# Second layer's prompt attention: the order of transposes and values on TensorE

## The reference, cut to what matters

```python
def dilated_prompt(q, k, v, slopes):
    outs, lses = [], []
    for gi, (w, r) in enumerate(B_PATTERNS):      # ((128, 1), (512, 4), (2048, 16))
        qs = to_sub(q[:, :, gi], r)[:, :, :, None]
        o, lse = banded_attention(qs, to_sub(k, r), to_sub(v, r), slopes[gi][:, None], r, w // r)
        ...
    return combine_groups(outs, lses)
# banded_attention, in blocks of 128 queries:
#   s = q k^T * HEAD_DIM**-0.5 - slope * distance, masked;  p = exp(s - lse);  o = p v
```

## Time and profile before

| | us |
|---|---|
| median of 3 runs | 2571.18 |
| lowest, highest | 2569.72, 2571.59 |
| the profiled execution | 2568.12 |
| its span | 2566.3 |
| TensorE busy (matmuls) | 2458.2 |
| VectorE busy | 1005.3 |
| ScalarE busy | 657.2 |

### The profile page before, as it was taken

One profiled execution on the slowest core, in us unless ns is written; L12 is line 12 of the kernel. 1 busy time (PEld: TensorE's weight loads), 2 busy tenths in 40 slices (PEclk: granted clock), 3 DMA queues, 4 the chain that ended last, 5 costly groups with the idle time before them and its releaser, 6 DMA issues. The chain is left out here.

```text
span 2566.3 us, 41256 instructions
## 1 busy us (share of the span) xinstructions
PE 2458.2 (96%) x16803; PEld 2369.6 (92%) x16803; DVE 1005.3 (39%) x1911; ACT 657.2 (26%) x1247; POOL 366.7 (14%) x242
## 2 busy tenths in 40 slices
PE   8999899999999999999999997689999999999997
PEld 8887799999999999999999775479999999999997
DVE  6566536322332232236212485436322322323235
ACT  4345324211110111123100493124211111111123
POOL 4333101101100101101111202201101100100100
PEclk9999999999999999999999999899999999999999
DMA  4011214113111313111211233523113111311312
GB/s 173 21 52 36 69 50 141 43 37 120 41 39 56 101 34 121 42 36 49 91 66 35 99 106 102 188 93 115 49 36 107 53 35 47 114 32 54 111 34 85
DMA packets 64943, 186.72 MB, mean 73 GB/s; under 512 B 11288, under 2 KB 17816, under 8 KB 64056
## 3 DMA queue, kind: packets, MB, share of 16 engines
q1 hardware_dynamic: 63928, 180.46, 21.7%
q0 software_dynamic: 912, 4.85, 0.5%
HBM read 175.85 MB, written 44.70 MB: 86 GB/s over the span
## 5 line engine op out<-in xcount | busy, mean ns | idle before, releaser
L969 DVE TENSOR_TENSOR WL<-RAW,WH 128x1024 fp32r<-128x1024 f32 (+3 forms) x196 | 216.4, 1105 | 1147.7 <-ACT WH L632 1147.1
L1508 PE MATMUL PS<-XH,WH 128*128 128x384 f32 x2832 | 621.0, 329 | 5.5 <-DVE XL L996 3.2
L1508 PE MATMUL PS<-XH,WL 128*128 128x384 f32 (+1 forms) x2736 | 603.5, 328 | 0.0
L1508 PE MATMUL PS<-XL,WH 128*128 128x384 f32 x2640 | 581.7, 328 | 0.0
L1508 PEld LDWEIGHTS PS<-XH,WH 128*128 128x128 f32 x2832 | 484.0, 188 | 7.3 <-issue 4.3
L632 ACT CAST WH<-RAW 128x1024 fp32r<-128x1024 f32 (+3 forms) x196 | 184.8, 944 | 1164.0 <-PE PS L1508 1149.1
L1508 PEld LDWEIGHTS PS<-XH,WL 128*128 128x128 f32 x2736 | 467.6, 188 | 0.0
L496 POOL TENSOR_TENSOR RAW<-RAW,GAIN 128x1024 f32<-128x1024 f32 x112 | 225.9, 2019 | 1663.7 <-DMA RAW<-in_w_gu 1418.7
L1508 PEld LDWEIGHTS PS<-XL,WH 128*128 128x128 f32 x2640 | 450.7, 188 | 0.0
L1508 PE MATMUL PS<-HL,WH 128*128 128x384 f32 (+1 forms) x1041 | 228.6, 327 | 0.0
L1508 PE MATMUL PS<-HH,WL 128*128 128x384 f32 (+1 forms) x1041 | 228.5, 327 | 0.0
(11 more groups left out here) (222 smaller groups left out, 2355.5 us busy)
## 6 DMA issues: line engine op xcount, KB each, us to landing
RAW<-in_w_gu SPq DMA_DIRECT2D x88, 512.0 KB, 3.5
out_bkS<-in_bk_in SPq DMA_DIRECT2D x8, 2032.0 KB
out_bvS<-in_bv_in SPq DMA_DIRECT2D x8, 2032.0 KB
RAW<-in_w_dn SPq DMA_DIRECT2D x32, 384.0 KB, 3.0
KC<-in_bk_in SPq DMA_DIRECT2D x8, 1536.0 KB, 10.9
VC<-in_bv_in SPq DMA_DIRECT2D x8, 1536.0 KB, 7.6
RAW<-in_w_dn SPq DMA_DIRECT2D x32, 320.0 KB, 2.9
XT<-in_xT SPq DMA_DIRECT2D x16, 544.0 KB, 4.8
```

The costliest lines, as they stand in the source:

```text
L969: nc.vector.tensor_tensor(lo[:, j, 0:nk * P], RAW[:, j, 0:nk * P], hi[:, j, 0:nk * P].bitcast(F32), ALU.subtract).then_inc(S["wl"], 1)
L1508: ins = mm(PS[:, 3 * j + c, 0:width], w[:, j, k * P:(k + 1) * P], x(k, a, width), start=(k == 0 and n == 0), stop=(k == nk - 1 and n == 2))
```

## The change

In each step of TensorE's loop the transposes of call s-2 now stand before the values of call s-3. VectorE's and ScalarE's orders, all waits, all buffers and all lags stay as they are.

```diff
             for s in range(C3 + V_LAG):
                 if s < C3:
                     scores_b(s)
+                if 0 <= s - T_LAG < C3:
+                    transposes_b(s - T_LAG)
                 if s >= V_LAG:
                     values_b(s - V_LAG)
-                if 0 <= s - T_LAG < C3:
-                    transposes_b(s - T_LAG)
```

## The result

The changed kernel takes 2577.89 us in the median of 10 runs, the kernel before 2571.95 in the median of 10: ratio 1.0023, 95% interval 1.0013 to 1.0033. It is slower by 5.9 us. The interval excludes a ratio of 1, but it doesn't lie wholly above 1.002, the line that the prediction drew. The profiled execution took 2575.40 us with a span of 2573.6, against 2568.12 and 2566.3: 7.3 more.

The account below looks back on a forecast made before the run. The loop around `PT` was taken as scarce, with TensorE nearly always busy. 1.75 (start and first stretch) + 1.68 (second) + 0.09 (third) + 1.17 (end) = +4.7 us; 2571.18 + 4.7 = 2575.9, range 2573.0 to 2579.5.

Parts of the forecast that it names:

- What bounds the loop: TensorE is busy 96% of the span; the scarce thing is the loop around `PT`: copy, values, next copy.
- Step (c), the block copy: On VectorE the block copy and `PT` copy both stand behind the values; each block copy costs 0.38 us, step 3.49.
- Effect (b): The cycle around `PT` keeps its members; the transposes' wait for `pev` is met at the same time as the values'.
- The start: At the loop's start, half 0 of the transposes runs ahead of ScalarE's copy: gain 0.51 us.
- The third group: Third stretch: steps of 3.55 us set by ScalarE become 3.49 as ScalarE works ahead; sum +0.09 us.
- Steps without a block copy: Transposes can start 1.87 us behind the values' start, 0.22 early; no cost, steps stay at 3.11.
- Effect (a): Transposes lose 1.02 us of cover from exponentials per call; 2.6 or 1.6 us are left, so cost nothing.
- Seams: On TensorE, scores directly behind values and transposes directly behind scores: taken as zero, upper bound +1.8 us.
- The shift behind the loop: The delay at the last values, +4.7 us, passes whole to the code behind the loop.
- The clock: Rival: stops of 0.38 us drop TensorE to 1.2 GHz for some 10 us, +9.3, 2585.2 us; chance 0.04.
- The block copy isn't in the way: Rival: VectorE finishes the block copy during TensorE's scores, only the start's gain is left, 2570.7 us; chance 0.08.
- The amplification: Rival: matmul hand-overs cost their bound or the sample attention meets its transfers worse, +6.5, 2577.7 us; chance 0.18.

Follow-up runs that it names:

- a_swap: Changed kernel, with VectorE's copy into `PT` moved ahead of the block copy of the same step: 2569.74 us, ratio 0.9995.
- a_late: Changed kernel, with VectorE doing each block copy one step later, still ahead of that step's `PT` copy: 2570.42 us, ratio 0.9999.
- a_half: Changed kernel, with the block copy taking 256 of its 512 columns: 2572.87 us, ratio 1.0005.
- a_wait: Changed kernel, with TensorE's transposes waiting for the copy out of the bank first and the exponentials second: 2576.56 us, ratio 1.0017.
- a_first: Changed kernel, with TensorE's new order in steps 0 to 15 only and the order of before from step 16: 2573.34 us, ratio 1.0009.
- a_swap_pv: a_swap, with VectorE's `PT` copy waiting for the end of the values first and the transposes second: 2569.22 us, ratio 0.9994.
- b_swap: Kernel before the change, with VectorE's copy into `PT` moved ahead of the block copy: 2571.02 us, ratio 1.0001.

## Why the prediction was right, and where it was off

The direction, the mechanism and the range held: the measured 2577.9 lies between 2573.0 and 2579.5. The likeliest value, 2575.9, was 2 us low; 0.8 of that is the base, 2571.18 in three runs and 2571.95 in ten. The outcome, +5.9 us, is just past the line of 5.1, on the side to which I had given 0.38; I had held the other, within 0.2%, for likelier (0.60). The working, stretch by stretch (us against before):

| stretch | predicted | measured |
|---|---|---|
| start (loop's begin to the scores of call 4) | -0.51 | -0.13 |
| first, 11 steps | +2.26 | +2.74 |
| second, 12 steps | +1.68 | +2.25 |
| third, 7 steps | +0.09 | +0.58 |
| end, to the last values | +1.17 | +1.42 |
| sum | +4.7 | +6.9 |

*What bounds the loop* was read rightly. The cover of the block copy was the crux, and a_swap, a_late and a_half show it from three sides.

*Step (c), the block copy.* The mechanism holds; the term was mis-sized. I put the chain at 1.13 + 0.60 + 0.74 + 1.02 = 3.49 us; it measures 1.15 + 0.60 + 0.83 + 1.00 = 3.58. The 0.74 was taken from a row where the `PT` copy releases the values, and used for the transposes. At the transposes the wait for that copy stands last of two, and that costs 0.09 more; a_wait takes it away again. Effect (b) made the same equation: it said that the transposes' wait for `pev` is met at the same time as that of the values. Some 0.08 us on each of 22 lengthened steps is 1.8 us of the 2.2 missing. That is more than the 1.3 that I had allowed for the hand-over. The range held it all the same, partly by luck: its upper end lies 3.6 above the likeliest value, about the sum of 0.6, 1.3 and the 1.8 for seams, and the seams cost nothing.

*The start.* The gain of 0.51 came out as 0.13 between these two executions, but what the order itself gives is steadier. It acts only behind the scores of call 3, and these rows of the changed kernel show how:

```profile
1448.57 1.13 PE L1815 MATMUL PS<-KB,QB 64*128 64x256 f32 x8
1450.79 0.57 ACT L859 COPY PT<-PS 128x512 f32<-128x512 f32 x1
1451.50 0.63 PE L1827 MATMUL PS<-IDN,SB 128*128 128x128 f32 x4 [1.21 <-ACT PT L859]
1452.06 1.09 PE L1844 MATMUL PS<-PT,VG 128*64 128x128 f32 x16
1453.09 1.13 PE L1815 MATMUL PS<-KB,QB 64*128 64x256 f32 x8
```

Half 0 of the transposes does run ahead of ScalarE's copy, as told; half 1 starts 0.71 behind that copy's start, and the values 0.56 later. From the scores of call 3 to those of call 4 it is 4.52 us; before the change it was 1452.68 - 1447.76 = 4.92, both at a clock of 1.00. The other four executions that have the new order here and a clock of 1.00 in this part (a_swap, a_late, a_half, a_first) show 4.50 or 4.51. So the gain is about 0.41, and 0.10 of the 0.51 was too much. The other 0.27 that is missing lies ahead of call 3's scores, where both kernels do the same in the same order: this part takes 7.65 us in the changed kernel, 7.38 before, and 7.26 to 7.57 in those four, with the clock below 1.00 at different moments (last section). That is a difference between executions, not an effect of the change.

*The third group* was to become faster per step, 3.49 instead of 3.55. With the true hand-over it is 3.57, just above the 3.55 that ScalarE alone would set. That the chain around `PT` sets it, and not ScalarE, is shown by a_wait: there the chain is shorter and the steps of the third group are 3.51, below 3.55. So ScalarE does work ahead, as told.

*Steps without a block copy* stay at 3.11, as said, but with less room than I gave them. Their transposes could start at V + 1.87 by my sum and at V + 2.05 by the measured hand-overs (1.22 + 0.83), against 2.09. In both hand-overs the wait in question stands last of two.

*Effect (a)*, the exponentials, costs nothing: a_swap has the same TensorE order and 34.25 us with no idle time. The waits view of the changed kernel does name ScalarE's exponentials ahead of the transposes six times, two of them at the start, as before; the other four are 1.6 us in all, which the prediction had listed as a sign of being wrong. In those four steps the transposes start 0.82 or 0.83 behind the `PT` copy, as in all others, and at the first (1505.02) the last exponentials of the call had started at 1501.06 and ended 0.49 later, 3.5 us before the transposes started. So the view names the wrong one of two semaphores there.

*Seams*: zero, the value taken, shown by the same 34.25.

*The shift behind the loop* passed through whole, as far as can be told: from the last values to the end it is 1006.2 us after and 1006.3 before. This part takes 1005.1 to 1009.1 us in the nine profiles, so the agreement to a tenth is chance in part.

*The rivals.* The clock stayed at 1.00 in all four stretches, although TensorE stands idle for some 0.4 us in each lengthened step that has scores. It was below 1.00 only in the loop's first part, and so it was before the change (0.55 until the scores of call 2, 0.60 before). The 10 us of low clock in that rival's price stood in no row. The Trainium skill (TensorE: Matmul & The Clock Gate, section A second HAM failure mode: psum-queue depth-cycling) tells of a kernel whose clock oscillates by short stops between groups of matmuls; this trace shows such stops and no oscillation. The gap of which the Trainium skill tells (VectorE: DVE Perf Modes, section The DRAIN you can't avoid) isn't seen either: it is 0.60 us from the block copy's start to the next in each step, which fits that section's exception, that an instruction which isn't held starts earlier. "The block copy isn't in the way" is wrong for the changed kernel and is just what a_swap makes true. The amplification did not occur either: no seam cost anything, and nothing grew behind the loop. That its 2577.7 is nearer to the measured 2577.9 than my likeliest value is a coincidence.

Neither a_swap (0.9995) nor a_swap_pv (0.9994) can be told from the kernel before by its time, though the trace shows 1.5 us less in a_swap's loop. TensorE's order makes no difference that the times could tell, if VectorE's order fits it; in the trace only the 0.41 us at the start are left of it.

## What to carry to other kernels

When work is reordered on one engine, look at what the other engines queue ahead of the copy that closes the cycle: a side job that was hidden because its input came early stops being hidden when its input becomes the last event. Take the cost from that chain, from start to start, each hand-over from a row with the same receiver and the same place among its waits. If the order on one engine changes, look whether the order on its partner has to change with it; here one exchange on VectorE gives back all of the loss.

## What the runs showed of the hardware

The wait that is met last cost more here when it stood behind another, already met one. TensorE's transposes start 0.83 us behind the start of the copy they wait for when that wait is second, 0.74 when it is first (a_wait). VectorE's copy starts 1.22 us behind the values' start when that wait is second, 1.14 when first (a_swap_pv). Two engines, 0.08 to 0.09 us each. Why isn't settled.

The clock at the loop's start isn't the same in every execution. In a_wait's profile the second part of the start ran at 0.57, and scores that take 1.13 us at 2.4 GHz took 2.08; in the changed kernel's profile it was the first part, at 0.66. TensorE had just stood idle for 2.3 us ahead of the loop, in these two and in the other seven profiles, so the idle time alone doesn't tell when the clock falls. The start took 12.8 us in the three executions with slow scores of call 3 (b_swap, a_wait, a_swap_pv) and 11.8 to 12.3 in the others. The window of a_wait (columns as above, the clock is third from the end):

```profile
1447.00:1454.92 7.92, 7.03 (x40) 5.14 (x40) 3.12 (x17) 6.90 (x29) 7.92 (x5) 0.57 1.05 404
```

The two windows of the changed kernel:

```profile
1440.92:1446.00 5.08, 4.59 (x32) 3.39 (x32) 3.14 (x24) 2.54 (x8) 5.02 (x4) 0.66 0.97 346
1446.00:1453.09 7.09, 4.55 (x41) 3.23 (x41) 3.56 (x19) 7.09 (x31) 7.09 (x5) 1.00 1.06 405
```

Outside the loop the same code took 2445.7 us in one profiled execution (a_late) and 2451.2 in another (a_wait). That spread of 5.5 us is nearly as large as the whole effect studied here, and it is why the distances inside the loop, which repeat to a hundredth, carry the argument.
